# Four of the second layer's modulation chunks moved from the first layer's mixer to its combining stage, and one ScalarE copy set behind other work

## The reference

```python
def _modulation(cond, w, b):
    return jax.nn.silu(cond) @ w + b

def _block(x, mod, mixer, ln, moe):
    sh1, sc1, g1, sh2, sc2, g2 = jnp.split(mod[:, None, :], 6, axis=-1)
    y, extras = mixer(x * (1.0 + sc1) + sh1)
    x = _layer_norm(DEEPNORM_ALPHA * x + g1 * y, ln[0], ln[1])
    x = _layer_norm(DEEPNORM_ALPHA * x + g2 * _hier_moe(x * (1.0 + sc2) + sh2, *moe), ln[2], ln[3])
```

## Time and profile before

| what | before |
|---|---|
| median of 3 runs (lowest to highest) | 1739.21 us (1736.78 to 1740.09) |
| the profiled execution's own time | 1740.79 us |
| its span | 1739.0 us |
| mean granted TensorE clock | 0.911 |
| PE busy | 1434.5 us, 82% of the span |
| PEld, DVE, ACT, POOL busy | 1085.4, 878.4, 630.9, 249.9 us |
| `late` products, L991 | 192 matmuls, from 322.3 to 445.5 us |

### The profile page before, as it was taken

The page is one execution under the profiler, slowest core; times in us unless marked ns, Lnnn a source line. Parts: engine busy times, 40 slices in busy tenths (PEclk is TensorE's granted clock), DMA queues, the critical chain, the costliest instruction groups (busy, mean ns, idle before and its releaser), DMA issues. The chain is left out here.

```text
span 1739.0 us, 22308 instructions
## 1 busy us (share of the span) xinstructions
PE 1434.5 (82%) x7723; PEld 1085.4 (62%) x7724; DVE 878.4 (51%) x1556; ACT 630.9 (36%) x1174; POOL 249.9 (14%) x229
## 2 busy tenths in 40 slices
PE   3799999687898999499993199989996894999960
PEld 0688888465566445487772188877885354777850
DVE  0422221535377263546655834528996555545538
ACT  0322221342344011257763422125553012665643
POOL 1100000111000031122222500010000121222215
PEclk9899999888999999599997599999997895999985
DMA  7344433556100820368994132210002602868763
GB/s 271 123 140 146 138 119 113 171 179 236 54 1 2 276 101 12 100 231 291 345 356 166 36 113 73 73 40 13 1 1 105 205 31 94 303 229 290 282 222 128
DMA packets 123492, 252.49 MB, mean 145 GB/s; under 512 B 18593, under 2 KB 51057, under 8 KB 123409
## 3 DMA queue, kind: packets, MB, share of 16 engines
q1 hardware_dynamic: 111296, 227.62, 38.6%
q0 software_dynamic: 12112, 23.77, 3.8%
HBM read 241.66 MB, written 29.61 MB: 156 GB/s over the span
## 5 line engine op out<-in xcount | busy, mean ns | idle before, releaser
L535 PE MATMUL psum<-in_parts 128*128 128x460 f32 (+2 forms) x1800 | 397.4, 381 | 23.2 <-PEq L336 23.2
L535 PEld LDWEIGHTS psum<-in_parts 128*128 128x128 f32 x1800 | 339.1, 189 | 85.5 <-issue 36.2
L2229 PE MATMUL psum<-moe_parts 128*128 128x256 f32 x1216 | 175.7, 298 | 1.5 <-ACT moe_parts L2273 1.5
L871 PE MATMUL psum<-layer 128*128 128x512 f32 x400 | 174.2, 595 | 2.7 <-PEq L797 2.7
L2229 PEld LDWEIGHTS psum<-moe_parts 128*128 128x128 f32 x1216 | 156.6, 195 | 19.5 <-issue 19.5
L767 DVE TENSOR_TENSOR moe_parts<-arena,moe_parts 128x1024 fp32r<-128x1024 f32 x128 | 151.4, 1223 | 30.0 <-ACT moe_parts L763 29.1
L572 DVE TENSOR_TENSOR in_parts<-in,in_parts 128x920 fp32r<-128x920 f32 (+2 forms) x54 | 62.5, 1158 | 192.6 <-ACT in_parts L567 192.6
L2247 PE MATMUL psum<-arena,moe 128*128 128x512 f32 x304 | 138.0, 596 | 0.0
L871 PEld LDWEIGHTS psum<-layer 128*128 128x128 f32 x400 | 75.9, 191 | 95.6 <-issue 94.1
L763 ACT CAST moe_parts<-arena 128x1024 fp32r<-128x1024 f32 x128 | 128.1, 1054 | 2.9 <-DMA arena<-in_moe_w 2.9
L567 ACT CAST in_parts<-in 128x920 fp32r<-128x920 f32 (+2 forms) x54 | 53.7, 994 | 191.9 <-PE psum L535 178.1
(11 more groups left out here) (316 smaller groups left out, 2100.1 us busy)
## 6 DMA issues: line engine op xcount, KB each, us to landing
arena<-in_moe_w SPq DMA_DIRECT2D x128, 512.0 KB, 8.7
arena<-in_moe_w SPq DMA_DIRECT2D x32, 1024.0 KB, 7.0
layer<-in_ada_w SPq DMA_DIRECT2D x24, 1024.0 KB, 6.4
in<-in_ada_w SPq DMA_DIRECT2D x16, 1024.0 KB, 5.8
in<-in_od_w_in SPq DMA_DIRECT2D x21, 512.0 KB, 3.6
arena<-y_rows SPq DMA_DIRECT2D x10, 1024.0 KB, 9.5
in<-in_ev_w_in SPq DMA_DIRECT2D x21, 460.0 KB, 3.5
start<-in_ada_w SPq DMA_DIRECT2D x8, 1024.0 KB, 15.8
```

The lines of the kernel that those rows point to most:

```text
L535: last = T.matmul(bank(g % W_BANKS)[:, 0:cw], a, b[:, kk], start=(k == 0 and m == 0), stop=(k == KD - 1 and m == 2))
L871: last = T.matmul(bank(g % 4), feats[k][:, t * P:(t + 1) * P], wout[:, k, j * BANK:(j + 1) * BANK], start=(k == 0), stop=(k == kt - 1))
L2229: T.matmul(UP[f][:, 0:2 * P], x_h[:, k, :], part_up(n, f)[:, k], start=(k == 0 and n == 0), stop=False)
```

## The change

Layer 1's twelve chunks are spread anew. Retention's first block makes two instead of three (`LATE1`), its second block still five (chunks 2 to 6), the preparation of latent attention one instead of four (chunk 7, ahead of item 0, picked after item 2). Chunks 8 to 11 move to `combine(0)`, in a second object of the class `Late` with four raw buffers: their first four transfers are issued by SP at the end of `experts(0)`, the other four in `combine(0)` behind the tile loads; PE does all products and picks there, ACT's copy of a chunk follows the normalising of a tile, and DVE keeps the four chunks and adds 1 to sc2 at the end. The rows of layer 1's modulation are turned, copied and written at the start of `differential_attention` instead of in `combine(0)`. Within retention's first block ACT now takes the Silu activations ahead of the second copy. The cut diff:

```diff
-LATE1, LATE2 = 3, 8
+LATE1, LATE2, LATE3 = 2, 7, 8
...
+            def __init__(self, name, i, chunks, raws, part):
+                self.i, self.chunks, self.ring = i, chunks, len(raws)
+                self.raw, self.part, self.top = [at(o, HK, ADA_CW) for o in raws], at(part, ADA_CW), raws[0]
+                self.landed = [sem(f"{name}_in{b}") for b in range(self.ring)]
+                self.used, self.copied, self.picked = sem(f"{name}_used"), sem(f"{name}_copied"), sem(f"{name}_picked")
...
+                if a >= self.ring:
+                    sp.wait_ge(self.used, a - self.ring + 1)
+                sp.dma_start(self.raw[a % self.ring], ada_source(self.i, self.chunks[a // 2], a % 2)).then_inc(self.landed[a % self.ring], 16)
...
-                n0, n1 = 4 * c0, 4 * c1
+                n0, n1 = 4 * self.chunks[c0], 4 * self.chunks[c1 - 1] + 4
...
-                    for c in range(LATE1):
-                        late.copy(act, c, SUMS)
+                    late.copy(act, 0, SUMS)
                     for t in range(NT):
                         A.activation(proj[:, t, RG:RG + RH * RDV], proj[:, t, RG:RG + RH * RDV], ACT.Silu)
+                    for c in range(1, LATE1):
+                        late.copy(act, c, SUMS)
                     act.drain()
...
-                    for a in range(2 * LATE1 + 2, 2 * LATE2 + 2):
+                    for a in range(2 * LATE1 + 2, min(2 * LATE2 + 2, 2 * LATE3)):
                         late.load(sp, a)
...
-            order = range(LATE2, ADA_CH)
-            MADE = dict(zip((0, 2, 4, 8), order))
-            TAKEN = dict(zip((0, 2, 4, 8), order))
+            MADE, TAKEN = {0: LATE2}, {0: LATE2}
...
-                    for a in range(2 * LATE2 + 2, 2 * ADA_CH):
+                    for a in range(2 * LATE2 + 2, 2 * LATE3):
                         late.load(sp, a)
...
-                    late.keep(dve, LATE2, ADA_CH, PICKED)
+                    late.keep(dve, LATE2, LATE3, PICKED)
                     dchain.join(dve)
-                    for s in (1, 4):
-                        m = modc[:, 1, s * KD:(s + 1) * KD, :]
-                        dchain.step(V.tensor_scalar(m, m, 1.0, None, ALU.add))
+                    scale1 = modc[:, 1, KD:2 * KD, :]
+                    dchain.step(V.tensor_scalar(scale1, scale1, 1.0, None, ALU.add))
...
                         if n == max(TAKEN) + 2:
-                            late.pick(pe, ADA_CH - 1, PICKED)
+                            late.pick(pe, LATE3 - 1, PICKED)
...
+            rowbuf = at(o + 2 * DH * DDV + 256, P)
+            rows_turned, rows_copied, rows_out = (sem(f"mod1_{n}") for n in ("turned", "copied", "out"))
...
                     sp.dma_start(lp, I["diff_lambda"][0].partition_broadcast(P)).then_inc(loaded, 16)
+                    sp.wait_ge(rows_copied, 1)
+                    sp.dma_start(mod_rows[1], rowbuf[0:2 * NMOD, :]).then_inc(rows_out, 16)
                     sp.dma_start(kc, I["cache_diff_k"][0, 0].rearrange("h p d -> p h d")).then_inc(k_in, 16)
...
+                    sp.wait_ge(rows_out, 16)
...
+                    act.wait_ge(rows_turned, 1)
+                    A.copy(rowbuf[0:2 * NMOD, :], bank(6)[0:2 * NMOD, 0:P]).then_inc(rows_copied, 1)
                     act.wait_ge(lam_v, 1)
...
+                    T.transpose(bank(6)[0:2 * NMOD, 0:P], modc[:, 1].rearrange("p n c -> p (n c)"), ident).then_inc(rows_turned, 1)
...
+                        elif n == 3:
+                            pe.wait_ge(rows_copied, 1)
...
+                    if late:
+                        for a in range(late.ring):
+                            late.load(sp, a)
...
-                if i + 1 < DEPTH:
+                if late:
                     @block.tensor
                     def _(pe):
-                        T.transpose(bank(0)[0:2 * NMOD, 0:P], modc[:, i + 1].rearrange("p n c -> p (n c)"), ident).then_inc(rows_turned, 1)
+                        for c in range(len(late.chunks)):
+                            if c:
+                                late.pick(pe, c - 1, bank(1))
+                            late.product(pe, 2 * c, bank(0))
+                            late.product(pe, 2 * c + 1, bank(0))
+                        late.pick(pe, len(late.chunks) - 1, bank(1))
 
...
-                    if i + 1 < DEPTH:
-                        sp.wait_ge(rows_copied, 1)
-                        sp.dma_start(mod_rows[i + 1], rowbuf[0:2 * NMOD, :]).then_inc(rows_out, 16)
-                        sp.wait_ge(rows_out, 16)
+                    if late:
+                        for a in range(late.ring, 2 * len(late.chunks)):
+                            late.load(sp, a)
...
-                    if i + 1 < DEPTH:
-                        act.wait_ge(rows_turned, 1)
-                        A.copy(rowbuf[0:2 * NMOD, :], bank(0)[0:2 * NMOD, 0:P]).then_inc(rows_copied, 1)
...
                             norm.normalise(act, t - 1)
+                            if late and t <= len(late.chunks):
+                                late.copy(act, t - 1, bank(0))
...
+                    if late:
+                        late.keep(dve, 0, len(late.chunks), bank(1))
+                        dchain.join(dve)
+                        scale2 = modc[:, i + 1, 4 * KD:5 * KD, :]
+                        dchain.step(V.tensor_scalar(scale2, scale2, 1.0, None, ALU.add))
+                        dve.drain()
...
-        late = Late(1)
+        late_at = ARENA - 2 * HK * ADA_CW - ADA_CW
+        late = Late("late", 1, range(0, LATE3), [late_at, late_at + HK * ADA_CW], ARENA - ADA_CW)
...
-        experts(0)
-        combine(0)
+        last = Late("last", 1, range(LATE3, ADA_CH), [R, R + HK * ADA_CW, R + 10000, R + 10000 + HK * ADA_CW], R + 10000 + 2 * HK * ADA_CW)
+        experts(0, last)
+        combine(0, last)
```

More of the change, by code:

```diff
@@ L990, in product @@
                 for k in range(HK):
-                    last = T.matmul(sums[32 * k:32 * k + 32, :], cond[:, half * HK + k, :], self.raw[a % self.RING][:, k],
+                    last = T.matmul(sums[32 * k:32 * k + 32, :], cond[:, half * HK + k, :], self.raw[a % self.ring][:, k],
                                     start=(half == 0), stop=(half == 1))
@@ L1011, in keep @@
                 dve.wait_ge(self.picked, c1)
-                n0, n1 = 4 * c0, 4 * c1
-                return dchain.step(V.tensor_tensor(modc[:, self.i, n0:n1, :], out[:, 2 * n0:2 * n1].rearrange("p (n c) -> p n c", c=2),
+                n0, n1 = 4 * self.chunks[c0], 4 * self.chunks[c1 - 1] + 4
+                return dchain.step(V.tensor_tensor(modc[:, self.i, n0:n1, :], out[:, 8 * c0:8 * c1].rearrange("p (n c) -> p n c", c=2),
                                                    bc(adab[:, self.i, n0:n1], 2, 2), ALU.add))
@@ L2086, in build, with experts @@
         XG = R + 6144
-        def experts(i):
+        def experts(i, late=None):
             o = XG
@@ L2347, in _, with combine @@
                     dve.drain()
-        def combine(i):
+        def combine(i, late=None):
             g2, gb = COMBINE
@@ L2356, in combine @@
             norm = Norm(f"l{i}_ln2", gb)
-            rows_turned, rows_copied, rows_out = (sem(f"mod{i + 1}_{n}") for n in ("turned", "copied", "out"))
-            rowbuf = at(R, P)
             with nc.Block(no_gpsimd_drain=True) as block:
-                if i + 1 < DEPTH:
+                if late:
                     @block.tensor
                     def _(pe):
-                        T.transpose(bank(0)[0:2 * NMOD, 0:P], modc[:, i + 1].rearrange("p n c -> p (n c)"), ident).then_inc(rows_turned, 1)
+                        for c in range(len(late.chunks)):
[4 more added lines that the diff above has]
+                        late.pick(pe, len(late.chunks) - 1, bank(1))
                 @block.sync
```

15 lines of the change are left out of this document (1 added, 14 removed).

## The result

| what | before | after |
|---|---|---|
| median of six runs each (lowest to highest), us | 1740.32 (1736.78 to 1745.17) | 1717.77 (1713.63 to 1720.55) |
| ratio after to before, 95% interval | | 0.9866 (0.9845 to 0.9888) |
| the profiled execution's own time, its span, us | 1740.79, 1739.0 | 1714.89, 1713.1 |
| mean granted TensorE clock | 0.911 | 0.916 |
| PE, DVE, ACT, POOL busy, us | 1434.5, 878.4, 630.9, 249.9 | 1438.1, 878.2, 630.9, 249.0 |

The account below looks back on a forecast made before the run. The prediction took the chain ending each block last as the bound, with 27.3 us of PE waits ahead of late products. Terms -11.7 - 11.3 + 0.5 + 0.5 = -22.0 us gave 1718 us, range 1712 to 1726.

Parts of the forecast that it names:

- Retention's first block, 11.7: One chunk fewer and Silu ahead of the second copy end the block 11.7 us earlier; bounds 8.1 to 12.1.
- Retention's second block, 0: Still five chunks at the same five places, now 2 to 6: no gain and no wait for chunk 2.
- The third rival: Retention's second block waits 2.86 us for each half of chunk 2: +5.7 us, 1724, chance 0.04.
- Latent preparation, 11.3: With three chunks removed there, the key products begin 11.3 us earlier; range 9.9 to 12.5.
- the clock should rise within the queries: Latent preparation: nearly unbroken PE work lifts the clock during the queries; a query costs 1.05 us at half, 0.61 at full.
- The rival of the slow clock: Latent preparation: clock stays low, queries 1.4 us longer, keys' first half doubles, together 7.3 us, 1725; chance 0.12.
- Experts' end, 0.5: Four loads added on SP's queue share the transfer engines with the last write-back: 0.5 us slower.
- a range to 6.3: Experts' end: write-back delay of 0 to 6.3 us; the rival takes 6.3 instead of 0.5, 1724, chance 0.15.
- its sign that the stretch should stay what it was: Experts' end: the time from the last write-back's issue to the tile loads should not change.
- Combining stage, 0.5: Four chunks added there cost 0.5 us with the joins, at worst 1; ACT's copies fit in 1.57 us of slack.
- the rival's 30: Combining stage: ACT's copies catch the chain and delay scaling and DVE: +30 us, 1748, chance 0.03.
- Differential attention, 0: Added turn, copy and write are hidden by DVE's 4.90 us lambda wait: nothing; without that cover 1 us.

Follow-up runs that it names:

- loads at the experts' start: Changed kernel with the four loads of chunks 8 and 9 issued ahead of all weights at the start of the experts' stage: 1720.69 us, ratio 0.9890.
- six chunks: Changed kernel with two more chunks moved: three in retention's second block, six in the combining stage: 1719.34 us, ratio 0.9879.
- GpSimd's spreading: Changed kernel with ACT copying the rotary key to one head only and GpSimd spreading it to the other seven: 1713.99 us, ratio 0.9841.
- both together: Changed kernel with GpSimd spreading the rotary key and chunk 8 made in the latent preparation ahead of item 5: 1717.06 us, ratio 0.9859.
- latent preparation alone: Retention as in the kernel before (three chunks, old ACT order, then five), no chunk in the latent preparation, four in the combining stage: 1730.86 us, ratio 0.9933.
- the last three runs: The chunk in the pause, GpSimd's spreading, and both together: 1716.29, 1713.99 and 1717.06 us.
- The run with the order alone: Kernel before with the Silu activations ahead of the copies of chunks 1 and 2 in retention's first block, no chunk moved: 1737.18 us, ratio 0.9977.
- the run with the old order: Changed kernel with both ACT copies again ahead of the five Silu activations in retention's first block: 1719.40 us, ratio 0.9876.
- the chunk in the pause: Changed kernel with chunk 8 made in the latent preparation where TensorE waits 2.38 us for ACT, three chunks in the combining stage: 1716.29 us, ratio 0.9851.
- the loads put late: Changed kernel with all eight loads issued in the combining stage behind the tile loads: 1720.70 us, ratio 0.9874.
- retention alone: Retention as in the changed kernel, four chunks in the latent preparation as before, one in the combining stage: 1726.55 us, ratio 0.9912.

## Why the prediction was right, point by point

The forecast was 1718 us, a gain of 22.0; the median is 1717.77, 22.6 below that of before. By the interval the gain lies between 19.5 and 27.0 us, so that the two agree within 1 is in part luck. At the places of the change the rows of the two profiles differ by 10.1 + 1.8 + 11.0 - 0.9 - 0.4 = 21.6 us.

- **Retention's first block, 11.7.** The chain was as forecast: copy, table, Silu, second copy, pick, `keep`. From the first copy to the end the forecast gave 344.85 - 335.46 = 9.4 us, measured 8.6. The difference is the pick: 1.05 us, not the 1.86 of the earlier trace rows, with a granted clock of 1.00 there; in four of the nine profiles with two chunks in that block (loads at the experts' start, six chunks, GpSimd's spreading, both together) it was 0.50, as in the forecast. From the copy on the block is 12.5 us shorter, but the two profiles have different starts, by 2.3 us, and with the longer one the state updates end 8.0 us behind the copy, with the shorter 8.8. Like compared with like, from DVE's first products to the block's end, the gain is the forecast's: with the longer start 44.7 us in the old code (latent preparation alone) and 33.0 with the change, 11.7 less; with the shorter 43.2 before and 31.1 to 31.5 in the last three runs, 11.7 to 12.1 less. The run with the order alone (4.0) and the run with the old order (Silu last again) show both parts of the term.
- **Retention's second block, 0.** Measured 1.8 better. Before, the second half of chunk 3 waited 1.13 us for its transfer, and the tile took 381.38 - 370.15 = 11.2 us; now none waits there and the tile takes 9.9. The three profiles with three chunks in the first block all have this wait, of 1.0 to 1.1 us, and the nine with two have none. Of the 1.8 this wait's 1.3 is the change's; the block as a whole took 56.5 to 58.0 us in the eight profiles that have its new five chunks. The third rival had looked for such a wait after the change; it was there before.

```profile
375.69 1.06 PE L991 MATMUL psum<-layer,arena 128*32 128x512 f32 x8 [1.13 <-DMA layer<-in_ada_w]
...
381.38 1.68 DVE L1277 BATCH_NORM_STATS2 layer<-psum 128x6 f32<-128x128 f32 x8 [5.27 <-PE psum L1190]
```

- **Latent preparation, 11.3.** Measured 11.0 from the first square to the keys. The working had one wrong step: "the clock should rise within the queries". Thirty query matmuls ran in 6.18 us, 1.03 a query, the half-clock price, where I had counted 4.9 for them. The third query started 0.7 us sooner than forecast after the key's data (6.3, not 7.0), since the key's turn took 0.86 in place of 1.52. The pause that I called "a little over 1 us" was 2.38. So the slow queries cost 1.3 us more than forecast, and the early start gave 0.7 of it back: that the term came out within 0.3 is partly luck.
- **The rival of the slow clock.** It came true for the queries. The keys did not cost double (the clock is 0.71 in 422 to 424 and 1.00 from 424). The heads behind them start at half clock and take 2.1 us longer than before, but that this is the change's doing is not shown: the run with Silu first, with the list of before there, loses 1.2 of it too (104.1 against 102.9), while all four profiles with the change's own preparation have 105.0. The Trainium skill's rule ("TensorE: Matmul & The Clock Gate", Part 1), that activity releases the clock, agrees with the chunk in the pause; with both edits TensorE was busy from 413.6 to 423.0 without a pause and stayed at 0.50. There activity alone did not release it, and the measurement decides: in this kernel the rule does not tell when the clock rises.

```profile
446.38 6.15 PE L1495 MATMUL psum<-layer 96*128 96x320 f32 x12 [1.99 <-PEq L1665]
```

- **Experts' end, 0.5.** Measured 0.9, and 0.0 to 2.0 over the seven profiles with the four loads there; with none or two there the stretch is 3.6 us, as before. The forecast took the near end of a range to 6.3 rightly; its sign that the stretch should stay what it was came true in one of the seven only (the old order on ACT). The Trainium skill's sentence that transfers from different engines interleave on the same engines ("DMA: Bandwidth & Descriptors", section "Issuing engines are not separate DMA queues") agrees with the first fetch, 4.3 us without and 7.6 with the loads beside it. The last write-back landed after 4.1 us, before after 3.2, by the rows of the transfers' view (after, then before):

```profile
y_rows<-moe POOLq DMA_INDIRECT x1, 4.1
```

```profile
y_rows<-moe POOLq DMA_INDIRECT x1, 3.2
```

  That is the 0.9 of the stretch. Over the seven profiles the write-back's landing runs from 3.2 us, where the stretch is 3.6, to 5.2, where it is 5.6.
- **Combining stage, 0.5.** DVE's chain is unchanged, 31.8 us, before 31.7, and the stage 0.4 longer. That ACT's copies can catch it is shown by the loads put late: 5.1 us on that chain and 4.2 on the stage, far below the rival's 30, since only the first chunk is late by much; at the next two copies ACT waits 1.59.
- **Differential attention, 0.** From the last matmul of layer 1's own projection to the first of its `mix_out` it took 177.3 us before (1164.3 to 1341.6) and 177.2 after (1139.9 to 1317.1).

What stays open is the clock: why the queries run at 0.50 with the change, and why the heads start slowly in some profiles and not in others. The larger gain of retention alone in the preparation goes with the clock and with 1.2 us less waiting for chunks; why both came out so is open too.

## What to carry to other kernels

Look at what a block ends with: an engine's list can hold work that waits for nothing behind copies that wait for transfers, and turning the two round gave 4 us here with no work moved. When work is moved to a stage whose engine is idle, start its loads before that stage; the same chunks with late loads made the stage 4.2 us longer, and the same loads put earlier held up another transfer by 3.3. Cost TensorE's work at both clocks: here the queries ran at 0.50 after work had been taken off, and the heads started at either clock with one and the same list of TensorE's ahead of them. Before a gain is read from two profiles, see whether the stretch begins alike in both.

## What the hardware showed that I had not expected

TensorE's clock in the preparation did not follow from its list alone. With the change it was 0.50 in 419 to 422, although TensorE worked without a pause from 417.59; with the chunk in the pause it was 0.98 in 416 to 419; with GpSimd's spreading 0.61 in 416 to 419; with both 0.50 from 413.6 to 423.0, 9.4 us of work without a pause. In the kernel before and in the run with Silu first TensorE's list is the same, and at the start of the heads its clock was 1.00 in the one (471.4 to 477.0) and at a mean of 0.71 in the other (466.1 to 472.0). This cost or gave 2 to 3 us in a block, more than two of the terms that I had summed. GpSimd spread 5376 elements on 32 partitions in 4.66 us, 0.87 ns each, where its product of 1024 elements on 128 partitions in retention takes 2.36 us, 2.3 ns each.
